# A decoder trunk: six column chunks of w_in multiplied k by k between the steps of the mixer, and mixer outputs in a held-back slot of the weight ring

## What is computed

```python
x = x + 0.5 * g1 * swiglu(modulate(rms_norm(x, ..), sh1, sc1), w_ffn1_in, w_ffn1_out)
u = modulate(rms_norm(x, ..), sh2, sc2) @ w_in          # 1024 x 2980
u_a, u_b, u_c, u_d = jnp.split(u, [OFF_LRU, OFF_HG, OFF_MLA], axis=-1)
y = concat(ssd_mixer(u_a), rglru_mixer(u_b), hgrn2_mixer(u_c), mla(u_d, paged_cache))
x = x + g2 * (rms_norm_per_head(y) @ w_out)
x = x + 0.5 * g3 * swiglu(modulate(rms_norm(x, ..), sh3, sc3), w_ffn2_in, w_ffn2_out)
```

## Time and profile before

| | us |
|---|---|
| median of 3 runs | 1918.91 (1913.8 to 1921.98) |
| the profiled execution | 1922.25 |
| its span | 1920.6 |
| busy: PE / DVE / ACT / POOL | 1722.7 / 957.4 / 610.7 / 236.5 |

### The profile page before, as it was taken

How to read it: one execution, slowest core, us unless ns; L and a number is a source line. 1 busy time by engine, 2 the same in 40 slices (tenths; PEclk the granted TensorE clock), 3 DMA queues, 4 the chain that set the end, 5 groups by cost and what they waited for, 6 DMA issues and landing times.

```text
span 1920.6 us, 27613 instructions
## 1 busy us (share of the span) xinstructions
PE 1722.7 (90%) x11256; PEld 1477.6 (77%) x11256; DVE 957.4 (50%) x1729; ACT 610.7 (32%) x972; POOL 236.5 (12%) x434
## 2 busy tenths in 40 slices
PE   5999999999767788999989999999977577899998
PEld 3999996667545557999979999967755465699998
DVE  3544432465776645344445444246667745444443
ACT  2433321033241324333334333111434223333331
POOL 7000003500044000000000000061004310000000
PEclk8999999999776799999999999999987677999999
DMA  9566647862011253554443554482301123435541
GB/s 319 186 198 201 210 145 216 277 207 87 1 53 42 93 207 117 167 164 153 155 156 132 175 160 153 146 254 87 101 15 43 33 62 132 132 132 175 165 148 67
DMA packets 206271, 272.00 MB, mean 142 GB/s; under 512 B 11778, under 2 KB 182238, under 8 KB 206144
## 3 DMA queue, kind: packets, MB, share of 16 engines
q1 hardware_dynamic: 188240, 236.90, 37.6%
q0 software_dynamic: 17904, 33.33, 6.1%
HBM read 264.68 MB, written 5.50 MB: 141 GB/s over the span
## 4 chain that ended last, share of the span: by engine, by line
PE 79%; DVE 14%; ACT 4%; issue 1%; DMA 1%; SPq 0%; ACTq 0%; DVEq 0%
PE bank L782 16%; PE bank L784 16%; PE bank L783 16%; PE bank L913 10%; PE bank L1294 4%; PE bank L1043 2%; PE bank L719 2%; PE bank L1209 2%; DVE sq L2254 2%; PE bank L709 1%; ACT sqk L1501 1%; DMA ring<-in_w_ada_dram 1%; DVE big L1980 1%; DVE zs L1613 1%; DVE big L2206 1%
## 5 line engine op out<-in xcount | busy, mean ns | idle before, releaser
L784 PE MATMUL bank<-hT_r,ring_r 128*128 128x320 f32 x1408 | 440.6, 313 | 0.0
L784 PEld LDWEIGHTS bank<-hT_r,ring_r 128*128 128x128 f32 x1408 | 267.6, 190 | 0.0
L1621 DVE TENSOR_TENSOR ring_r<-ring,lat_pages_r 128x2048 fp32r<-128x2048 f32 (+1 forms) x68 | 151.4, 2230 | 160.4 <-ACT lat_pages_r L1320 160.3
L782 PE MATMUL bank<-hT_r,lat_pages_r 128*128 128x320 f32 x704 | 218.8, 311 | 13.5 <-DVE gates_r L1653 13.5
L783 PE MATMUL bank<-gates_r,lat_pages_r 128*128 128x320 f32 x704 | 219.7, 312 | 0.0
L784 PE MATMUL bank<-big_r,ring_r 128*128 128x320 f32 x704 | 218.0, 310 | 0.0
L913 PE MATMUL bank<-hT,ring 128*128 128x320 f32 x736 | 211.2, 445 | 4.7 <-DVE hT L1647 4.7
L913 PEld LDWEIGHTS bank<-hT,ring 128*128 128x128 f32 x736 | 141.9, 195 | 65.9 <-issue 12.6
L1320 ACT ACTIVATE lat_pages_r<-ring 128x2048 fp32r<-128x2048 f32 (+1 forms) x68 | 126.4, 1862 | 140.7 <-DMA ring<-in_w_ffn_in_dram 66.2
L782 PEld LDWEIGHTS bank<-hT_r,lat_pages_r 128*128 128x128 f32 x704 | 134.2, 191 | 18.5 <-issue 18.5
L783 PEld LDWEIGHTS bank<-gates_r,lat_pages_r 128*128 128x128 f32 x704 | 134.0, 190 | 0.0
(11 more groups left out here) (534 smaller groups left out, 3150.8 us busy)
## 6 DMA issues: line engine op xcount, KB each, us to landing
ring<-in_w_ffn_in_dram SPq DMA_DIRECT2D x88, 1024.0 KB, 6.2
ring<-in_w_ada_dram SPq DMA_DIRECT2D x60, 1024.0 KB, 6.1
ring<-in_w_ffn_out_dram SPq DMA_DIRECT2D x32, 1024.0 KB, 5.2
ring<-in_w_in_dram SPq DMA_DIRECT2D x22, 1024.0 KB, 7.1
sqk<-in_w_ada_dram POOLq DMA_DIRECT2D x24, 512.0 KB, 7.1
ring<-in_w_ffn_out_dram SPq DMA_DIRECT2D x16, 768.0 KB, 4.3
lat_pages<-in_cache_mla_latent_dram POOLq DMA_DIRECT2D x128, 64.0 KB, 2.2
ring<-in_w_out_dram SPq DMA_DIRECT2D x8, 1024.0 KB, 8.7
```

The costliest lines, as they stand in the source:

```text
L782: mm(out, w_h, x_h, start=start, stop=False)
L784: return mm(out, w_l, x_h, start=False, stop=stop)
L1621: go(v.tensor_tensor(slot_r(n, nk, 256), slot(n, nk, 256), w_hi_r[g % HI][:, 0:nk].bitcast(F32), ALU.subtract), w_low)
```

## The change

1. Six chunks, q, iv and g (numbers 19 to 24, from `FILL0` = 19), no longer run in `win`. Their 48 matmuls per layer are dealt out by `fill(n)` between the steps of the mixers: ten places with four matmuls, then two behind each of the first four steps of the HGRN2 loop. `WIN` and `WCH` are reordered: fz comes ahead of gate and q.
2. They all go to bank 7. So attention over the pages has banks 4 and 5 only (`n % 2`), and chunk i starts once chunk i - 1 has been taken out.
3. `hT` must live on for the chunks. The outputs of SSD, HGRN2 and MLA go to a slot of the ring, those of RG-LRU (later than before, after the last chunk) to `hT[:, 2:4]`. `hold` marks the slot ahead of w_in tile 9. Until all of `w_out` is multiplied, `place_tile` passes it over, and the next tile for it waits for `wo_done` = 8.
4. The transposed tails and the decay sums move ahead of the softmax transposes and the product by v of the prompt; `out27` moves to `vg`. On DVE the decay steps and the copies follow. On ACT `att_copy(2)` moves ahead of the square root of RG-LRU, and `take` of the six chunks moves in among the squares.

```diff
+        def hold(key, *free):
+            pos[key] = len(tl)
+            held[:] = [len(tl) % RING, free]
+
+        def skip_held():
+            if held[0] == len(tl) % RING:
+                tl.append((None, 0, 0, *held[1]))
...
+                if t == WCH[FILL0][2]:
+                    hold(("mixed", l), wo_done, (l + 1) * KD)
...
+                    if src is None:
+                        sp.sem_inc(slot_loaded[n % RING], 16)
+                        continue
...
-                    for i in range(21, 24):
-                        win(i)
...
+                    fills = iter([(i, k) for i in range(FILL0, len(WCH)) for k in range(KD)])
+                    def fill(n):
+                        for i, k in itertools.islice(fills, n):
+                            _, _, t, c0 = WCH[i]
+                            if k == 0:
+                                tile_ready(pe, pos["win", l, t])
+                                if i == FILL0:
+                                    pe.wait_ge(att_q, at(att_q, 1))
+                                else:
+                                    pe.wait_ge(*taken(i - 1))
+                            w = slot(pos["win", l, t], 8, WIN[t][1])
+                            ins = mm(bank[7][:, 0:T], w[:, k, c0:c0 + P], hT[:, k], start=k == 0, stop=k == KD - 1)
+                            if k == KD - 1:
+                                ins.then_inc(win_done, 1)
...
-                            if i >= 3:
-                                pe.wait_ge(att_sq, at(att_sq, n - 2))
-                            mm(bank[(4, 5, 7)[n % 3]][:, 0:288], latT[:, i], wkq, start=True, stop=True).then_inc(att_k, 1)
+                            if i >= 2:
+                                pe.wait_ge(att_sq, at(att_sq, n - 1))
+                            mm(bank[4 + n % 2][:, 0:288], latT[:, i], wkq, start=True, stop=True).then_inc(att_k, 1)
+                            if 0 < i <= fills_in:
+                                fill(1)
...
@@ DVE, behind turned_states(1)
+                    ve.wait_ge(stored_rows, at(stored_rows, 16 * N_STORE_ROWS))
+                    take(21)
```

More of the change, by code:

```diff
@@ L531, in trunk @@
                            8, 256, wo_done, l * KD + 2 * t + 2)
+            held[0] = None
             place_ffn(2 * l + 1)
@@ L538, in slot_r, with win_bank, mixer_out @@
             return carve(as_r["ring"], (n % RING) * SLOT, chunks, width)
+        def win_bank(i):
+            return bank[7 if i >= FILL0 else i % 3]
+        def mixer_out(l):
+            slot_now = carve(ring, (pos["mixed", l] % RING) * SLOT, 3, 2, T)
+            return [slot_now[:, 0], hT[:, 2:4], slot_now[:, 1], slot_now[:, 2]]
         def tile_ready(eng, n):
@@ L963, in _ @@
                     ins.then_inc(mla_pe, 1)
-                    for i in range(15, 18):
-                        win(i)
+                    win(15)
+                    win(16)
                     pe.wait_ge(mla_dve, at(mla_dve, 5))
                     mm(bank[7][:, 0:T], c("rot"), qr, start=True, stop=True).then_inc(mla_pe, 1)
-                    win(18)
-                    win(19)
+                    for i in range(17, FILL0):
+                        win(i)
+                    if WCH[FILL0 - 1][2] in WIN_STEP[l]:
+                        ada_turn(WIN_STEP[l][WCH[FILL0 - 1][2]])
                     pe.wait_ge(mla_dve, at(mla_dve, 6))
@@ L984, in _ @@
                     ins.then_inc(mla_pe, 1)
-                    win(20)
+                    pe.wait_ge(conv_done, at(conv_done, 1))
+                    for i in range(FILL0 - 3, FILL0):
+                        pe.wait_ge(*taken(i))
+                    for k in range(KD):
+                        ins = pe.transpose(bank[k // 4][0:27, (k % 4) * P:(k % 4 + 1) * P], last_cols[:, k], c("ident"))
+                    ins.then_inc(turned, 1)
                     pe.wait_ge(mla_dve, at(mla_dve, 7))
@@ L989, in _ @@
                     ins.then_inc(mla_pe, 1)
-                    for i in range(21, 24):
-                        win(i)
+                    fills = iter([(i, k) for i in range(FILL0, len(WCH)) for k in range(KD)])
[12 more added lines that the diff above has]
+                                ins.then_inc(win_done, 1)
+                    fill(4)
+                    pe.wait_ge(ssd_dve, at(ssd_dve, 1))
+                    pe.wait_ge(turned_used, at(turned_used, 2))
+                    pe.wait_ge(mod_ready, max(WIN_STEP[l].values()) + 1)
+                    for cc, (t0, L) in enumerate(TC):
+                        ca = c("causal") if cc < 2 else c("causal_s", 64)
+                        la_ = c("later") if cc < 2 else c("later_s", 64)
+                        for h in range(4):
+                            mm(bank[cc][0:L, h * L:(h + 1) * L], dta[0:L, cc, h:h + 1].to_broadcast([L, L]), ca,
+                               start=True, stop=True)
+                        mm(bank[3][0:L, 4 * cc:4 * cc + 4], ca, dta[0:L, cc], start=True, stop=True)
+                        ins = mm(bank[3][0:L, 12 + 4 * cc:16 + 4 * cc], la_, dta[0:L, cc], start=True, stop=True)
+                        for h in range(4 if cc else 0):
+                            r = slice(64 * (h % 2), 64 * (h % 2) + 64)
+                            c0 = 24 + 192 * (h // 2) + t0 - P
+                            ins = mm(bank[3][r, c0:c0 + L], dta[0:L, cc, h:h + 1].to_broadcast([L, 64]), ca, start=True, stop=True)
+                    ins.then_inc(ssd_pe, 1)
                     pe.wait_ge(mla_dve, at(mla_dve, 8))
@@ L997, in _ @@
                     ins.then_inc(mla_pe, 1)
-                    win(24)
+                    fill(4)
                     pe.wait_ge(mla_dve, at(mla_dve, 9))
@@ L1159, in _ @@
                     turn(2)
-                    score(2)
+                    fill(4)
+                    score(2, 4)
                     pe.wait_ge(lru_act, at(lru_act, 3))
@@ L1181, in _ @@
                         ins.then_inc(hg_bc, 1)
+                        fill(2)
                         if d == 1:
@@ L1435, in _ @@
                     modulate(1)
+                    mixer = mixer_out(l)
                     def take(i):
@@ L1523, in _ @@
                     att_squares(0)
+                    take(20)
                     att_root(0)
@@ L1545, in _ @@
                     att_root(3)
+                    take(24)
                     soft_exp(1)
@@ L1954, in _ @@
                         go(v.tensor_scalar(bht_out(qrep[:, :, g]), bht(bank[4][:, 0:256]), c("rows32")[:, g:g + 1], None, MUL))
+                    ve.wait_ge(ssd_act, at(ssd_act, 2))
+                    softplus(0, 12)
+                    do(v.tensor_copy(dtv.rearrange("p a b -> p (a b)"), sp[3][:, 0:12]))
+                    do(v.scalar_tensor_tensor(dta, dtv, -1.0, aneg.unsqueeze(1).to_broadcast([P, 3, 4]), MUL, MUL), ssd_dve)
+                    ve.wait_ge(turned, at(turned, 2))
+                    go(v.tensor_copy(out27[0:27, 0:512], bank[0][0:27, :]))
+                    do(v.tensor_copy(out27[0:27, 512:1024], bank[1][0:27, :]), turned_used)
+                    o.tell(out_ready)
                     ve.wait_ge(prob_act, at(prob_act, 8))
```

125 lines of the change are left out of this document (52 added, 73 removed), and 4 rows, old and new, of the table WCH.

## The result

The changed kernel takes **1943.88 us** (median of 4 runs, 1942.97 to 1949.13); the kernel before, with one more run, 1920.45. The ratio is 1.0143, with a 95% interval of 1.0124 to 1.0161. The forecast was 1939 in a range of 1914 to 1952, slower by 20 where the medians differ by 23. The ratio says a little more than the medians (1943.88 / 1920.45 is 1.0122): 1920.45 is the median of only four executions, the kernel before stood at 1916.5 to 1917.1 in the three later measurements, and a ratio of 1.0143 to that is 27 us more. Run again later, beside the experiments, the changed kernel took 1947.91 and its ratio was 1.0158 (1.0139 to 1.0176).

What follows compares the result with a forecast made beforehand. PE was taken to bound the projection, with 65 us of its time idle in the mixers. Layer 1's +3.4, layer 0's +1.4 and the FFN's -2 x 12.5 made 20.2 us slower: 1939 us, range 1914 to 1952.

Steps and rivals of the forecast that it cites:

- I: Into the second FFN: its first tiles queue on SP behind the w_ada tile awaiting wo_done 8; 12.5 us lost per layer.
- A: Projection: five chunks leave the path ahead of the decay sums, 17.4 us gained per layer.
- B: Behind the decay sums: fills, softmax transposes, score copies and product by v slip onto the path; about 6.9 us lost.
- C and D: score(0) with two banks and four fills, 0.9 us lost; second fill at turn(1) waiting for DVE's take(21), 2.6 lost.
- E to H: Later mixers: fills ahead of L1124 gain 1.8 us, fills inside score(1) lose 0.9; then F, G and H.
- H: Clock: new idle gaps ahead of the prompt's scores and decay sums drop pieces to half clock; 2.5 us lost per layer.
- G: RG-LRU product moved behind the HGRN2 loop, 0.8 us lost; two banks in later scores, 2.2 lost; 3.0 together.
- F: ACT ahead of score(2): att_copy(2) comes earlier, but take(23) may bring another table load; net 1.0 us gained.
- The first: Rival: fills keep PE's clock up through the mixers, so the result is not slower, 1914 us; chance 0.16.
- The second: Rival: chunks are free, mixers keep 17.4 us per layer and the FFN loses only 9.3, 1903 us; chance 0.09.
- The third: Rival: nothing is won in the mixers, the six chunks cost what they did before, 1951 us; chance 0.2.
- The fourth: Rival: loads waiting for wo_done 8 land early enough, leaving only the mixers' gain, 1914 us; chance 0.05.

Runs made afterwards that it cites:

- e2: Kernel before, with one more SP wait holding the second w_ada tile ahead of the second FFN until wo_done 8: 1940.97 us, ratio 1.0126.
- e1: Changed kernel with the held slot released behind the second w_ada tile, so the FFN's first tile is no longer late: 1921.49 us, ratio 1.0029.
- e3: Changed kernel with DVE's take(21) moved from behind the second block of transposed states to within the step before it: 1939.06 us, ratio 1.0120.
- d2: c2 with three banks in turn again for the page scores from the fifth sequence on: 1912.05 us, ratio 0.9980.
- c2: c1 plus ACT's take(23) moved behind the copy of the fourth sequence: 1909.38 us, ratio 0.9963; measured again 1911.03, ratio 0.9973.
- c1: Changed kernel with the edits of e1 and e3 together: 1916.73 us, ratio 0.9993.
- e4: Changed kernel with only the first and last of each chunk's eight matmuls, 36 per layer left out (results not the reference's): 1941.64 us, ratio 1.0128.
- c3: c2 plus all eight matmuls of chunk 19 run in PE's idle time ahead of the decay sums: 1915.54 us, ratio 0.9997.
- d1: c2 with the page transposes of turn(0) and four fill matmuls moved behind the transposes for SSD on PE: 1915.55 us, ratio 0.9995.

## Why the prediction was right, point by point

- **I, the FFN's late start.** Forecast 12.5 per layer; the trace gives 12.9 in layer 0 and 13.0 in layer 1 (end of `w_out` to the first FFN product), e2 24.5 for both by itself. The chain was as forecast step by step: landing 8.2 behind T0 (8.3 forecast), the residual's end at T0 + 13.25 (13.6). PE's waits up to the first FFN product are 17.4 us, where I had written about 19. This term carries the sign, and e1 and e2 show it in both directions. That the three FFN tiles only queue behind a tile that waits was the reading that mattered, and it stands in SP's order, not in the diff.
- **A.** Forecast 17.4 with the decay sums 125.6 us into layer 1 (1376.3 - 1250.7); measured 17.3 and 125.7. PE's idle ahead of the prompt's scores became 4.2 (4.4 forecast) and ahead of the decay sums 5.0.
- **B** was too small: 6.9 forecast (its own terms, 9.5 less 2.26, make 7.2), 10.8 measured in layer 1, 8.7 in layer 0. I took the slipped steps at full clock and side by side. They run at half clock in part (2.04 for 1.13, 3.67 for 2.39), and the copy behind the decay steps holds PE for another 1.9.
- **C and D.** Forecast 3.5 together; measured 6.5 ahead going down to 2.4, so 4.1, of which D is 3.5 (forecast 2.6). e3 shows D: 3.6 at its place, 5 to 9 in the whole.
- **E to H** were forecast to take the lead from 7.0 to 3.4, -3.6 together; in the trace of layer 1 it goes from 2.4 to 3.3, so +0.9. Part of H had been paid in B, where the clock fell. G's banks are worth nothing that can be seen (d2). Where `take(23)` stands, a part of F, does cost: moving it took 7.3 us off (c2 against c1, expected 3 to 4), though the intervals allow for less and c2's second measurement puts it at about 4. That this is the table loads is my reading; their number did not change.
- **Layer 0's tail.** Forecast 2.0 late; the two waits for tiles are 2.6, and the way from there to `w_out` is 3.0 longer.
- **The sum.** Mixers and tail together were forecast at +3.4 and +1.4; the first profile has +3.3 and +2.6, and the two layers as a whole lose 20.0 there, 20.2 by the forecast. This agreement is luck: B is off by 4 in one direction and E to H by 4.5 in the other, and leads of this size vary from one execution to the next. The changed kernel's second profile has +3.2 in layer 1 but -1.1 in layer 0, and e2, with the old mixers, has +3.4 and +1.1. The runs say that the sign of this part was wrong. With each kernel set against the kernel before on its own chip, the change without the late tile costs 0.29% in e1 (interval 0.19 to 0.40), 0.17% as the first ratio less that of e2, and 0.32% as the second: 3 to 6 us lost, where I had forecast 4.8 gained. Only the bare medians of the first measurement make it 1 gained (23.4 against 24.5), and they lean on the 1920.45. So the call and the bulk of the size come from I, which was right step by step; A to H and the tail did not earn their share.
- **The rivals.** The first (the clock stays up) had a cause that exists, since the mixers' granted clock rose from 0.73 to 0.81 by the windows below, but the end did not come nearer by that, and it is no 10 us per layer. The second (the chunks are free, 1903) falls with the 13 us of I and the gain given back; e4 bears out only that leaving the chunks out hardly moves the end. The third (nothing is won, 1951) is nearer to the changed kernel's second measurement (1947.91) than the forecast is, and by e1 and e2 it is right about the mixers. The fourth is refuted by the 16.37 of ACT.

Busy time by stretch in layer 1, the projection up to the decay sums and the mixers up to `w_out` (columns as above), in the kernel before:

```profile
1250.70:1393.70 143.00, 139.51 (x608) 100.02 (x609) 82.60 (x207) 33.81 (x56) 42.24 (x78) 0.98 0.49 147
1393.70:1621.60 227.90, 163.67 (x1192) 118.48 (x1192) 151.51 (x346) 74.02 (x204) 43.25 (x78) 0.73 0.19 58
```

and in the changed kernel:

```profile
1263.00:1389.00 126.00, 114.33 (x484) 81.63 (x485) 78.17 (x200) 28.21 (x49) 42.47 (x78) 0.95 0.46 135
1389.00:1631.00 242.00, 185.16 (x1317) 130.67 (x1317) 155.95 (x354) 82.41 (x213) 43.25 (x78) 0.81 0.22 67
```

The projection is 17 us shorter with 25 us less of PE in it, the mixers are 14 longer with 21 more. PE's idle in the two together is 3.5 + 64.2 = 67.7 us before and 11.7 + 56.8 = 68.5 after. The work moved, and the idle stayed. That it is time in which DVE and ACT have PE's inputs in hand, and not room that PE fails to use, is what the rows suggest; no run shows it for each step, and in e4, where the end hardly moved, the clock changed as well.

What stays open: what the moved steps and the clock each give back. Filling the gap (c3) and taking the steps out of the way (d1) each moved their own place and not the median. Also open is what the six chunks cost at an equal clock, and why the changed kernel's two medians differ by 4 us; the passage with two clocks is a candidate of the right size, but no run holds the clock fixed. The best version here is c2 (the changed kernel with three repairs), 0.9963 and 0.9973 of the kernel before in two measurements. It beats the kernel before by 6 to 8 us and the changed kernel by over 30.

## What to carry to other kernels

When a change holds back a buffer, follow the next load that is to go there and everything behind it in the issuing engine's order: loads whose own slots are free are late as well, and one wait more on SP, passed once in each layer, cost 24.5 us here (e2). Before counting an engine's idle time as room, look for what the other engines do in it: 52 us of PE's work were moved into PE's idle time here, and nothing was won. That the moved steps joined the chain of the others is the likely reason, shown for one of them (e3) and not for the row behind the decay sums. And put a take-out that a later fill waits for ahead of work that nobody waits for as early: that was worth 5 to 9 us (e3).

## What the runs showed of the hardware that I had not expected

The same stretch of the same instructions, after 3.3 to 5.0 us of idle on PE, was granted 0.90, 0.87, 0.68 and 0.67 of full clock in four executions and took 16.6 to 20.4 us. In two of them PE stayed at half clock for some 13 us, though it was busy for all of nine microseconds in the middle (c1). Leaving out 39 us of matmuls in the mixers (e4) moved the time by 2 to 6 us, with the mixers' granted clock down from 0.81 to 0.77. A table load on ACT takes 1.28 us, and the next activation can follow 0.02 behind it; timeline of ACT in c1:

```profile
1467.92 1.28 ACT L1503 ACT_TABLE_LOAD   x1
1469.22 0.44 ACT L1503 ACTIVATE vg<-bank 128x320 f32<-128x320 f32 x1
```
